# Sums of squares for six norms in a two-layer encoder step: two rounded products in place of one full-precision product

## What is computed

```python
def rmsnorm(x, g):
    xf = x.astype(jnp.float32)
    y = xf * lax.rsqrt(jnp.mean(xf * xf, axis=-1, keepdims=True) + EPS)
    return (y * g.astype(jnp.float32)).astype(x.dtype)
...
for i in range(DEPTH):
    h = rmsnorm(x, norm_mix[i])
    # layer 0: gMLP and Mamba-2 mix, layer 1: retention; x = x + mix
    h = rmsnorm(x, norm_ffn[i])
    x = x + conv_ffn(h, ...)
    gate = jax.nn.sigmoid(rmsnorm(x, norm_ple[i]) @ ple_w_gate[i])
    x = x + gate * (p[i] @ ple_w_proj[i])
x = rmsnorm(x, norm_final)
```

## Time and profile before

| | |
|---|---|
| median of 3 runs | 1807.99 us (1806.44 to 1808.13) |
| the profiled execution | 1806.36 us, span 1804.6 us |
| TensorE busy | 1787.1 us, 99% of the span |
| VectorE, ScalarE, GpSimd busy | 940.5, 637.9, 831.7 us (52, 35, 46%) |
| mean granted TensorE clock | 0.994 of full |
| DMA | 161.04 MB, 89 GB/s |

### The profile page before, as it was taken

One profiled execution on the slowest core, in us unless ns is written; L12 is line 12 of the kernel. 1 busy time (PEld: TensorE's weight loads), 2 busy tenths in 40 slices (PEclk: granted clock), 3 DMA queues, 4 the chain that ended last, 5 costly groups with the idle time before them and its releaser, 6 DMA issues.

```text
span 1804.6 us, 34101 instructions
## 1 busy us (share of the span) xinstructions
PE 1787.1 (99%) x13949; PEld 1745.5 (97%) x13949; DVE 940.5 (52%) x1510; ACT 637.9 (35%) x986; POOL 831.7 (46%) x410
## 2 busy tenths in 40 slices
PE   9999999999999999999999999999999999999997
PEld 8999989999999999999999999999899999999997
DVE  6578776666515524556444441444555425515465
ACT  6335564442212312344433331333333222312342
POOL 4333323675535544576433334333465535544563
PEclk9999999999999999999999999999999999999998
DMA  6222332222342222232222222222222222322231
GB/s 236 83 75 84 94 94 72 91 85 86 114 141 82 92 95 91 67 111 82 86 80 74 72 76 84 77 80 80 68 81 94 83 93 82 103 85 84 65 98 50
DMA packets 58533, 161.04 MB, mean 89 GB/s; under 512 B 6833, under 2 KB 19121, under 8 KB 58433
## 3 DMA queue, kind: packets, MB, share of 16 engines
q1 hardware_dynamic: 52368, 151.03, 25.9%
q10 hardware_dynamic: 6064, 8.61, 1.4%
HBM read 153.94 MB, written 5.67 MB: 88 GB/s over the span
## 4 chain that ended last, share of the span: by engine, by line
PE 91%; issue 3%; DVE 3%; POOL 2%; ACT 0%; DMA 0%; DVEq 0%; POOLq 0%; SPq 0%
PE proj L321 81%; PE Q L1054 5%; PE proj L1054 2%; POOL w_lo L417 1%; PE Q L1349 0%; DMA w_raw<-in_w_v 0%; POOL arena L620 0%; PE Q L1280 0%; DVE arena L1925 0%; ACT arena L670 0%; PE Q L1234 0%; POOL arena L663 0%; DVE rstd L372 0%; PE Q L1081 0%; PE Q L333 0%
## 5 line engine op out<-in xcount | busy, mean ns | idle before, releaser
L417 POOL TENSOR_TENSOR w_lo<-w_raw,w_hi 128x1024 fp32r<-128x1024 f32 (+2 forms) x276 | 660.8, 2395 | 762.8 <-ACT w_hi L343 745.2
L321 PE MATMUL proj<-op_hi,w_hi 128*128 128x256 f32 x4208 | 881.1, 291 | 1.9 <-DVE op_lo L1536 0.8
L321 PE MATMUL proj<-op_hi,w_lo 128*128 128x256 f32 x4208 | 870.3, 288 | 0.0
L321 PE MATMUL proj<-op_lo,w_hi 128*128 128x256 f32 x4208 | 863.2, 286 | 0.0
L321 PEld LDWEIGHTS proj<-op_hi,w_hi 128*128 128x128 f32 x4208 | 672.8, 188 | 17.0 <-issue 12.4
L321 PEld LDWEIGHTS proj<-op_lo,w_hi 128*128 128x128 f32 x4208 | 675.4, 188 | 0.0
L321 PEld LDWEIGHTS proj<-op_hi,w_lo 128*128 128x128 f32 x4208 | 671.5, 188 | 0.0
L343 ACT ACTIVATE w_hi<-w_raw 128x1024 fp32r<-128x1024 f32 (+2 forms) x275 | 283.6, 1031 | 654.3 <-PE proj L321 648.8
L1606 DVE TENSOR_TENSOR arena<-proj,rstd 128x512 f32<-128x512 f32 x141 | 97.5, 691 | 209.9 <-PE proj L321 199.8
L1613 DVE TENSOR_TENSOR x<-proj,x 128x512 f32<-128x512 f32 x72 | 49.7, 690 | 240.7 <-PE proj L321 240.7
L670 ACT ACTIVATE arena<-arena 128x128 f32<-128x128 f32 (+6 forms) x298 | 129.1, 475 | 59.7 <-DVE arena L1609 29.8
(11 more groups left out here) (193 smaller groups left out, 1010.5 us busy)
## 6 DMA issues: line engine op xcount, KB each, us to landing
w_raw<-in_w_gu SPq DMA_DIRECT2D x88, 512.0 KB, 3.4
w_raw<-in_w_down SPq DMA_DIRECT2D x32, 512.0 KB, 3.4
w_raw<-in_w_heads_a SPq DMA_DIRECT2D x30, 512.0 KB, 3.4
w_raw<-in_w_heads_b SPq DMA_DIRECT2D x18, 512.0 KB, 3.4
w_raw<-in_w_gate SPq DMA_DIRECT2D x16, 512.0 KB, 3.4
w_raw<-in_w_xbc SPq DMA_DIRECT2D x12, 512.0 KB, 3.4
w_raw<-in_w_down SPq DMA_DIRECT2D x16, 384.0 KB, 3.0
w_raw<-in_w_u SPq DMA_DIRECT2D x8, 512.0 KB, 3.5
```

Of the source, the lines that this page charges most:

```text
L321: last = nc.tensor.matmul(proj[:, 2 * g.mod(2) + half, 0:size], w[:, lo:lo + P], o[:, at:at + size], start=(k == 0 and j == 0), stop=(k == ...
L417: nc.gpsimd.tensor_tensor(w_lo[:, c:c + width], w_raw[:, c:c + width], w_hi[:, c:c + width], ALU.subtract).then_inc(w_lo_done, 1)
```

## The change

For the six norms after the first, `ssq` is split like an operand before it is multiplied with ones: ScalarE rounds it into `sums` (high part), VectorE subtracts to get the low part, and TensorE runs four rounded matmuls, two passes of two halves, in place of two full-precision ones. `sums` lies over the buffer of the squares, and `ones_r` (rounded ones) over the dt weights; it is made once, by ScalarE during the u phase. The diff:

```diff
+        sums = nc.alloc_sbuf_tensor_at("sums", [P, 2 * T], R, offset=nc.sbuf_base)
         sq = sb("sq", 2 * T)
...
+        ones_r = nc.alloc_sbuf_tensor_at("ones_r", [P, P], R, offset=nc.sbuf_base)
         w_dt = sb("w_dt", 8 * SH)
...
         def mean_square(pe, name, free=()):
 
-            pe.wait_ge(nsem("ssq"), ncount(name, "ssq", KD))
             for s_, v_ in free:
                 pe.wait_ge(s_, v_)
+            if name != "n_in":
+                pe.wait_ge(sem("sums_lo"), NORMS.index(name))
+                for j in range(2):
+                    nc.tensor.matmul(Q[:, 2, 0:HALF], ones_r[:, :], sums[:, j * T:j * T + HALF], start=(j == 0),
+                                     stop=(j == 1))
+                    last = nc.tensor.matmul(Q[:, 3, 0:HALF + TS], ones_r[:, :], sums[:, j * T + HALF:(j + 1) * T],
+                                            start=(j == 0), stop=(j == 1))
+                last.then_inc(nsem("ms"), 1)
+                return
+            pe.wait_ge(nsem("ssq"), ncount(name, "ssq", KD))
             nc.tensor.matmul(Q[:, 2, 0:HALF], ones[:, :], ssq[:, 0:HALF], start=True, stop=True)
             nc.tensor.matmul(Q[:, 3, 0:HALF + TS], ones[:, :], ssq[:, HALF:T], start=True, stop=True)\
                 .then_inc(nsem("ms"), 1)
...
         def act_root(act, name):
+            if name != "n_in":
+                act.wait_ge(nsem("ssq"), ncount(name, "ssq", KD))
+                nc.scalar.activation(sums[:, 0:T], ssq[:, :], ACT.Copy).then_inc(sem("sums_hi"), 1)
             act.wait_ge(nsem("ms"), ncount(name, "ms", 1))
...
         def dve_rstd(dve, name):
+            if name != "n_in":
+                dve.wait_ge(sem("sums_hi"), NORMS.index(name))
+                nc.vector.tensor_tensor(sums[:, T:2 * T], ssq[:, :], sums[:, 0:T], ALU.subtract).then_inc(sem("sums_lo"), 1)
             dve.wait_ge(nsem("root"), ncount(name, "root", 1))
...
                 if n == 5:
+                    act.wait_ge(sem("wdt_lo"), 1)
+                    run(ones_r[:, :], ones[:, :], ACT.Copy, "ones_r")
                     act.wait_ge(sem("cs_copied"), 1)
```

## The result

The changed kernel takes 1826.19 us in the median of five runs (1825.58 to 1828.24), against 1806.44 us (1803.92 to 1808.13) for the kernel before in five. The ratio is 1.0112, with a 95% interval of 1.0101 to 1.0124: slower by 1.1%, some 20 us. A second comparison later gave 1.0115 (1.0100 to 1.0131).

What follows compares the result with a forecast made beforehand. TensorE, busy 99% of the span, was taken to bound the kernel. Stalls 17.65, restarts 0.6, saving 2.5 off: +15.7; clock +4.0: 19.7 us on 1806.36, plus 1.6 for the median: 1827.7 us, range 1820 to 1832.

Steps and rivals of the forecast that it cites:

- What TensorE saves: At each of six norms, four rounded matmuls take 0.50 in place of 0.92 us: 0.42 saved, 2.5 in all.
- The stalls: TensorE waits at six norms for rounding, subtraction and hand-offs, 17.65 us in all, 5.21 at each ple norm.
- The second rival: At n_yb and n_mix1 VectorE doesn't wait for GpSimd: 2.9 us less, 1824.8; chance 0.09.
- Restarts: After each of six waits, TensorE's first pair takes 0.1 us more: 0.6 in all.
- Edits at nothing: Rounded ones, root, reciprocal and clearing of ssq cost nothing; nothing new becomes last elsewhere, and nothing gives the stalls back.
- The clock: Granted clock falls at both long ple stalls; bounds 0 and 3.0 us each, 2.0 taken, +4.0 in all.
- The third rival: The clock falls at the shorter stalls of 2.3 and 2.5 us too: 2 x 2.0 more, 1831.7; chance 0.11.
- The first rival: The clock holds, or falls and returns within the stalls: 1823.7; chance 0.27.
- The sum: Whole kernel: 15.7 + 4.0 = 19.7 us on the profiled 1806.36, giving 1826.1, and 1827.7 for the median.
- The rule on idleness: Skill's rule against long TensorE idleness, read as only idleness counts: sum stays as is, third rival drops out.

Runs made afterwards that it cites:

- the kernel without the waits: Against the kernel before: GpSimd's last addition writes the rounded type, no split, four rounded matmuls going twice over the high part; 1803.12 us, ratio 0.9981.
- the filled stall: Against the changed kernel: TensorE runs ten unused full-precision matmuls before each of the two ple waits; 1822.20 us, ratio 1.0084 to the kernel before.

## Why the prediction was right

The forecast was 1827.7 us, slower by 1.1%; the medians measured were 1826.19 and 1827.28. The 1.6 us that the forecast added for the median of three runs before didn't last: the median of five is 1806.44, and without that term the forecast is 1826.1. That the total came out so close is partly luck. The mechanism is the forecast one, but the term of the clock was too small, and the clock elsewhere in the program (at n_yb, near 220 us, at the end) moves single executions by a microsecond or two.

*What TensorE saves.* 0.42 a norm, 0.43 read in the kernel without the waits. 2.5 us in all stands.

*The stalls*, each read as TensorE's start less its last pair's start and 0.25:

| | forecast us | measured us |
|---|---|---|
| n_yb | 2.25 | 2.24 |
| n_ffn0 | 1.37 | 1.35 |
| n_ple0 | 5.21 | 5.15 |
| n_mix1 | 2.53 | 2.51 |
| n_ffn1 | 1.08 | 1.14 |
| n_ple1 | 5.21 | 5.15 |
| sum | 17.65 | 17.54 |

The causes of the large ones were tested. Moving the subtraction (and the rounding) ahead in the programs shortened the ple stalls; keeping GpSimd out brought the subtraction at n_yb from 2.18 back to 0.72. The two FFN stalls, of 1.35 and 1.14, are the plain length of rounding, subtraction and hand-offs and only the run without the subtraction bears on them. The second rival, that VectorE doesn't wait for GpSimd, falls.

*Restarts.* 0.11 each: four matmuls from 356.83 to the next slab at 357.44 are 0.61 and not 0.50.

*Edits at nothing.* They held. The third slab after n_mix1 waits 0.3 us for the first output tile as before. Stretches between the norms that hold no fall are as long as before within 0.2 us once product and restart are allowed for, so nothing gave the stalls back.

*The clock.* This was the term taken between 0 and 3.0 for each long stall, and 2.0 was chosen. It fell at both, and cost 2.4 and 2.8: the term was 1.2 too small in all. The third rival, a fall at the shorter stalls too, is half true: it came at n_yb in five of the six profiles of kernels with that stall of 2.2 us, and cost 1.5 where it was measured; it was absent in the first profile of the change. The first rival, that the clock holds, would have given 1823.7 and is refuted by the stretches at 0.50 and by the filled stall.

*The sum* on the profiled executions: 17.54 + 0.66 - 2.5 + 5.2 = 20.9. The two profiles are 21.9 apart. TensorE had already arrived at n_yb 1.7 us late (354.59 against 352.87), ahead of any of the six products: near 220 us, where the earlier trace rows show a fall that both kernels have, the lower clock lasted longer in this execution. The same stretches after:

```profile
216.00:222.00 6.00, 5.74 (x42) 3.77 (x40) 5.49 (x10) 0.91 (x4) 0.00 (x0) 0.76 0.74 235
222.00:226.00 4.00, 4.00 (x19) 3.30 (x19) 2.62 (x11) 3.94 (x9) 0.00 (x0) 0.50 0.16 47
226.00:230.00 4.00, 4.00 (x22) 4.00 (x22) 0.13 (x2) 1.21 (x3) 2.36 (x1) 0.59 0.00 0
```

At a mean of 0.76, 0.50 and 0.59, 2.9 + 4.0 + 3.3 = 10.2 us of them were at half, against 6.8 before. This varies from execution to execution: in the thirteen profiles, whose programs are the same here but for one short operation at 112 us, the time at half clock near 220 us is 3.4, 6.8 or 10.2 us. It is therefore not put down to the change. With these 1.7 us added and the 0.45 of the shorter end taken off, the sum is 22.2 against 21.9; 0.3 stays unexplained. The kernel before varies from 1803.9 to 1808.1 by itself.

*The rule on idleness.* The Trainium skill, "TensorE: Matmul & The Clock Gate", section "Why this matters for your kernels", says that long idle gaps between bursts of matmuls bring the lower rate. The filled stall agrees for the two long ones: the same wait, no idleness, no fall. The rows of the other places don't: the clock fell at a stall of 2.2 us, where by the forecast's reading of the rule the third rival should have dropped out, and near 220 us with TensorE busy for 5.74 of 6.00 us. The rows decide.

## What to carry to other kernels

Before an operation is put in front of a busy engine, look up where its inputs are made in the other engines' programs: a step appended to a function that nobody was waiting for yet inherits everything queued ahead of it, here 3.6 us of low parts. Then price a cheaper instruction against the hand-offs it needs; 0.4 us on the bound engine doesn't pay for two dependent operations of 0.7 us unless the consumer arrives 1.5 us after their input. A stall of several microseconds on TensorE has to be charged with the clock behind it as well, here about half as much again (2.4 and 2.8 us on 5.15).

## What was not expected of the hardware

The clock can fall at a stall of only 2.2 us (n_yb, five profiles of six), and in two profiles (the kernel with the earlier split at the ple norms, and the one with the filled stalls) it also fell at n_mix1, where TensorE stood for 2.5; in the change's first profile it did at neither. Whether it falls at such a stall differs between executions of the same program, and the runs don't say what decides it. And matmuls whose results nobody reads, put into a stall that couldn't be avoided, took 4 us off the kernel.
